# A depthwise convolution's partial sums for two of four channel tiles, added by accumulating transfers within SBUF in place of GpSimd additions

## The reference

```python
proj = h @ w_in
glu_in, qkv, gates = jnp.split(proj, [2 * CONV_WIDTH, 2 * CONV_WIDTH + 3 * ATT_WIDTH], axis=-1)
u_val, u_gate = jnp.split(glu_in, 2, axis=-1)
u = u_val * jax.nn.sigmoid(u_gate)
u = causal_depthwise_conv(u, conv_w, conv_b)      # 31 taps, 512 channels
u = jax.nn.silu(layernorm(u, conv_ln_g, conv_ln_b))
y_conv = u @ w_conv_out
...
o = stick_breaking_attention(qkv[:, :, 0], qkv[:, :, 1], qkv[:, :, 2])
...
merged = jax.nn.sigmoid(g_conv) * y_conv + jax.nn.sigmoid(g_att) * y_att
```

## Time and profile before

| | |
|---|---|
| time before, median of 3 runs | 1374.23 us (1372.99 to 1374.35) |
| profiled execution | 1373.22 us, span 1371.4 us |
| PE busy in the span | 1344.5 us (98%) |
| DVE busy | 986.8 us (72%) |
| ACT busy | 714.9 us (52%) |
| POOL busy | 180.9 us (13%), of it 105.7 us in the 60 sums |
| mean granted TensorE clock | 0.996 |

### The profile page before, as it was taken

The page is one execution under the profiler, slowest core; times in us unless marked ns, Lnnn a source line. Parts: engine busy times, 40 slices in busy tenths (PEclk is TensorE's granted clock), DMA queues, the critical chain, the costliest instruction groups (busy, mean ns, idle before and its releaser), DMA issues.

```text
span 1371.4 us, 19821 instructions
## 1 busy us (share of the span) xinstructions
PE 1344.5 (98%) x7788; PEld 1170.3 (85%) x7788; DVE 986.8 (72%) x1390; ACT 714.9 (52%) x1170; POOL 180.9 (13%) x167
## 2 busy tenths in 40 slices
PE   9999999999999999999999999999999999999997
PEld 7888888788769999998887778887778999998885
DVE  6799899678587878878326764677787788776322
ACT  4466886553475555573224543557465555564221
POOL 3388343200010000004000011121000000000000
PEclk9999999999999999999999999999999999999998
DMA  9422112455701332324532144543221323333221
GB/s 368 146 92 93 47 47 77 148 183 184 299 16 62 100 117 93 122 94 155 176 100 89 62 127 121 133 112 89 95 74 34 121 93 117 100 108 108 92 92 62
DMA packets 45310, 155.98 MB, mean 114 GB/s; under 512 B 6049, under 2 KB 6305, under 8 KB 45090
## 3 DMA queue, kind: packets, MB, share of 16 engines
q1 hardware_dynamic: 42882, 149.70, 32.9%
q0 software_dynamic: 2336, 5.01, 1.6%
HBM read 143.39 MB, written 2.10 MB: 106 GB/s over the span
## 4 chain that ended last, share of the span: by engine, by line
PE 88%; DVE 7%; ACT 3%; issue 1%; POOL 0%; DVEq 0%; ACTq 0%; POOLq 0%
PE ps L1741 27%; PE ps L1742 26%; PE ps L1743 26%; PE ps L1891 1%; DVE t_buf L1098 1%; PE ps L1829 1%; DVE w_lo L1064 1%; PE ps L2157 1%; PE ps L1783 1%; PE ps L1794 1%; PE ps L1795 1%; PE ps L1799 1%; DVE h_lo L1090 1%; ACT w_hi L578 1%; PE ps L2125 0%
## 5 line engine op out<-in xcount | busy, mean ns | idle before, releaser
L1741 PE MATMUL ps<-h_hi,w_hi 128*128 128x256 f32 (+1 forms) x1120 | 374.0, 334 | 3.0 <-ACT sq L806 1.1
L1743 PE MATMUL ps<-h_hi,w_lo 128*128 128x256 f32 (+1 forms) x1120 | 371.6, 332 | 0.0
L1742 PE MATMUL ps<-h_lo,w_hi 128*128 128x256 f32 (+1 forms) x1120 | 371.4, 332 | 0.0
L1064 DVE TENSOR_TENSOR w_lo<-raw,w_hi 128x1024 fp32r<-128x1024 f32 x141 | 183.7, 1306 | 115.6 <-ACT w_hi L578 114.4
L1741 PEld LDWEIGHTS ps<-h_hi,w_hi 128*128 128x128 f32 x1120 | 212.8, 190 | 27.1 <-issue 3.5
L1743 PEld LDWEIGHTS ps<-h_hi,w_lo 128*128 128x128 f32 x1120 | 212.8, 190 | 20.3
L1742 PEld LDWEIGHTS ps<-h_lo,w_hi 128*128 128x128 f32 x1120 | 212.9, 190 | 19.4 <-issue 0.5
L578 ACT ACTIVATE w_hi<-raw 128x1024 fp32r<-128x1024 f32 x141 | 148.1, 1055 | 147.1 <-PE ps L1743 74.0
L1054 DVE TENSOR_TENSOR w_lo<-quads,w_hi 128x1024 fp32r<-128x1024 f32 (+1 forms) x152 | 164.8, 1085 | 72.7 <-ACT w_hi L578 72.7
L578 ACT ACTIVATE w_hi<-quads 128x1024 fp32r<-128x1024 f32 (+1 forms) x152 | 144.3, 949 | 78.2 <-PE ps L1743 76.6
L1741 PE MATMUL ps<-act_hi,w_hi 128*128 128x512 f32 x352 | 137.0, 389 | 0.0
(11 more groups left out here) (316 smaller groups left out, 2262.3 us busy)
## 6 DMA issues: line engine op xcount, KB each, us to landing
quads<-in_ffn_in SPq DMA_DIRECT2D x76, 512.0 KB, 4.5
raw<-in_ffn_out SPq DMA_DIRECT2D x44, 512.0 KB, 3.7
raw<-in_ada SPq DMA_DIRECT2D x32, 512.0 KB, 4.2
raw<-in_qk SPq DMA_DIRECT2D x25, 512.0 KB, 3.7
ada<-in_ada SPq DMA_DIRECT2D x16, 512.0 KB, 7.6
raw<-in_gates SPq DMA_DIRECT2D x16, 512.0 KB, 3.7
raw<-in_v SPq DMA_DIRECT2D x12, 512.0 KB, 3.7
raw<-in_ffn_in SPq DMA_DIRECT2D x12, 512.0 KB, 3.9
```

Source lines behind the costliest of these rows:

```text
L1064: nc.vector.tensor_tensor(w_lo[SLOT[p]][:], raw[q % RAW][:], w_hi[SLOT[p]][:].bitcast(f32), ALU.subtract).then_inc(raw_used, 1)
L1741: nc.tensor.matmul(out, w[0], v[0], start=start, stop=False, **kw)
L1742: nc.tensor.matmul(out, w[0], v[1], start=False, stop=False, **kw)
L1743: return nc.tensor.matmul(out, w[1], v[0], start=False, stop=stop, **kw)
```

## The change

POOL no longer adds. For each of the 60 sums it issues a transfer from `tap_buf` to `conv`, both in SBUF, that adds what it brings to what stands there. The one counter `pool_tap` becomes two, `tap_sum[0]` for even n and `tap_sum[1]` for odd n, each raised by 16 when a transfer has landed; the same three waits (POOL's for the sum two places before, ACT's for the sum three places before, PE's for all sums) go to them. Order and number of the products, the three buffers and all other work stay.

```diff
-        mod_one, mod_ready, pool_tap = sem("mod_one"), sem("mod_ready"), sem("pool_tap")
+        mod_one, mod_ready = sem("mod_one"), sem("mod_ready")
+        tap_sum = [sem(f"tap_sum{i}") for i in range(2)]
...
             for n, (c, j) in enumerate(SUM_ORDER):
                 pool.wait_ge(tap_prod, n + 3)
                 if n >= 2:
-                    pool.wait_ge(pool_tap, n - 1)
-                nc.gpsimd.tensor_tensor(conv[:, c, :], conv[:, c, :], tap_buf[n % 3][:], ALU.add).then_inc(pool_tap, 1)
+                    pool.wait_ge(tap_sum[n % 2], 16 * (n // 2))
+                nc.gpsimd.dma_start(conv[:, c, :], tap_buf[n % 3][:], accum_op=ALU.add).then_inc(tap_sum[n % 2], 16)
...
                 for c, j in SUM_ORDER[tapped[0]:tapped[0] + n]:
                     if tapped[0] >= 3:
-                        act.wait_ge(pool_tap, tapped[0] - 2)
+                        act.wait_ge(tap_sum[(tapped[0] - 3) % 2], 16 * ((tapped[0] - 3) // 2 + 1))
...
                     pe.wait_ge(tap, len(TAP_ORDER))
-                    pe.wait_ge(pool_tap, len(SUM_ORDER))
+                    for i in range(2):
+                        pe.wait_ge(tap_sum[i], 16 * (len(SUM_ORDER) // 2))
```

## The result

The changed kernel takes 1404.37 us (median of 4 runs, 1398.62 to 1406.17) against 1373.64 us before (4 runs, 1372.99 to 1374.35): 2.2% slower, ratio 1.0216, 95% interval 1.0186 to 1.0247. The prediction was 1381.4 us, with a range from 1371.5 to 1399, so the result lies outside it. The sign was right and the size was not: the loss is 30.7 us where 7.2 were forecast.

What follows compares the result with a forecast made beforehand. PE was taken as the bound. -1.7 (wait for `qk_lo`) + 7.2 (late scores(1)) + 1.7 (clock) = +7.2 us on 1373.22 gave 1380.4; the runs' median, 1.0 higher, made it 1381.4, range 1371.5 to 1399.

Steps and rivals of the forecast that it cites:

- What bounds the kernel, and what can be gained: PE, busy 98% of the span, is the bound; only its 1.7 us wait for `qk_lo` can be gained.
- L: One link: time from an accumulating transfer's start of issue to the earliest issue of the next on the same tile.
- L alone, 3.9 us: Link of an undisturbed adding transfer, with 1.58 us of engine time charged for two passes: 3.9 us.
- L beside loads, 4.4 us: Link with two sums in flight and panels' loads holding 0.28 of the DMA engines: 4.4 us.
- a landing of 4.1 us: Sign in POOL's issue rows for `conv`: 4.1 us to land (L less 0.3) if the forecast is right.
- What L costs: In qk1 and v1, ACT falls behind; scores(1) begins at 83.8 + 14 L, 145.4 instead of 138.22: +7.2 us.
- The tail, hidden until L = 4.7: Last three sums on the odd tile end at 253.9, ahead of the mean at 254.81: no cost below L = 4.7.
- The clock, 1.7 us: Two new PE waits may cost one dip to half clock: between 0 and 3.4 us, 1.7 taken.
- hidden: Rival: L at most 4.0, adding costs no second engine pass, only DVE's relief is left: 1372.5 us, chance 0.36.
- The engines are the bound: Rival: DMA engines or POOL's issue bound, L 5.5 or more; at 5.6, 1401 us; chance 0.10.
- relief: DVE's taps, no longer slowed beside POOL's additions, end PE's wait for `qk_lo`: -1.7 us.
- the forecast's own formula: Start of scores(1) at 83.8 + 14 L us; each 0.1 us of L beyond 3.9 costs 1.4 us.

Runs made afterwards that it cites:

- experiment 3: Sums 33 to 53 by adding transfers, all others by GpSimd's additions as in the kernel before: 1371.87 us (11 runs), ratio 0.9987.
- experiment 2: The changed kernel with the panels from qk1 2 to gates 15 loaded in only 16 of 1024 columns: 1378.17 us in one run.
- experiment 8: The changed kernel with copies instead of additions and the loads from qk1 2 to gates 15 cut to 16 columns: 1373.83 us in one run.
- experiment 6: The changed kernel with 40 products of ones on PE right ahead of its wait for the last sums: 1403.0 us in one run.

## Why the prediction was right in sign and wrong in size

- **What bounds the kernel, and what can be gained:** right. PE's wait for `qk_lo` was the only gain, and it was half of what was forecast, 0.9 us for 1.7: DVE, freed of 2.3 us, next waits 1.3 us for ACT's `w_hi` (experiment 3).
- **L alone, 3.9 us:** right. It is 3.8 (experiment 2). The charge of 1.58 us of engine time for an adding transfer had the right size too: the page of the kernel before has, for the software queue,

```profile
q0 software_dynamic: 2336, 5.01, 1.6%
```

  so that in experiment 2 the 60 sums took 8.3% of 16 x 1376.3 us less 1.6% of 16 x 1371.4, which is 1477 us, or 1.54 us for each sum and engine, where 1.58 was forecast. A copy takes 0.69 (experiment 8, the same way, with a span of 1372.0 us). That the longer time is a second pass is not shown: the queue's bytes are the same for both, but an addition takes 144 packets, (10976 - 2336) / 60, and a copy 80, (7136 - 2336) / 60, so the smaller packets may be the reason as well. The 2.0 us plus bytes that the Trainium skill gives (DMA: Bandwidth & Descriptors, Anatomy of one DMA, SWDGE path), an estimate of 2.6 us here, lies between the landing of a copy (2.3 in experiment 8) and that of an addition (3.3 in experiment 2); the adding itself is not in it.
- **L beside loads, 4.4 us:** this is the step that failed. The trace has 5.0 over the first 11 links. 4.4 was the engine time that two sums need at a given share of loads, taken as the mean of L. That is only a floor for the rate; a transfer that meets a 512 KB load is late by itself (5.8 us to land from 91.55, with a load at 91.60, against 3.3 us in experiment 2), and the next sum of its tile cannot start meanwhile. Links of 3.8 to 7.0 us stand side by side. A mean share also takes the loads to be spread evenly, and they come in step with the sums. The sign that the prediction had named for being right, a landing of 4.1 us, is met by the page's median of 4.2: a median over all 60 hides the long ones, of up to 7.2 us.
- **What L costs:** the slope was right (14 links up to scores(1)). Between +7.2 and the 17.9 measured (19.4 less 1.5 of the start) 10.7 us were missed. Of these the first 11 links, at 4.97 for 4.4, are 6.3. The three behind the restart are 3.5: from the second sum of the pair (137.10 + 0.6) to product 32 at 154.41 they take 16.7 us, 5.6 each, where 13.2 were forecast. Some 0.9 are small steps between. The pair at the restart stands beside a load at 137.47; experiment 2 shows a long link at the same place with hardly any bytes of loads.
- **The tail, hidden until L = 4.7:** the limit was right, and L was over it: 263.06 + 0.6 to 283.5, three links of about 6.6 us. SP issues a load 0.4 to 0.5 us behind each of these three sums (264.04, 271.98 and 277.76), and in experiment 2, with few bytes of loads, the mean does not wait. 5.7 us for 0.
- **The clock, 1.7 us:** mis-sized: 4.5 behind scores(1) and 3.1 behind the mean, 7.6 in all. The second is shown to come from the wait (experiment 6), the first is read from the clock alone. The lower clock ahead of scores(1), 0.80 from 111 to 136 us, adds nothing to that: it lies inside the 17.9 us, and PE still had to wait at the end of them.
- **The rivals:** "hidden" fell. "The engines are the bound", with L = 5.6 and 1401 us, had the size, at a chance of 0.10, partly by luck: it had scores(1) at +24.0 us, where 17.9 were measured, and the tail and the clock too low, 2.7 and 1.7 for 5.7 and 7.6. But its reason, that loads and sums delay each other, is what the trace shows.

The mechanism was thus right, and the term that was mis-sized is L beside loads: 5.0 us over the first 11 links, 5.6 at the restart and 6.6 in the tail, for 4.4. Of the 30.3 us of the profile without the start's 1.5, 23.1 were missed: 10.7 up to scores(1), 5.7 in the tail, 5.9 of clock behind the two waits, and 0.8 of relief that did not come. By the forecast's own formula the mean of the 14 links, L = 5.1, gives 155.2 for scores(1), +17.0 us; with the tail's 5.7, the clock's 7.6 and the relief's 0.9 us it comes to +29.4.

## What to carry to other kernels

A chain of dependent transfers is priced by its slowest links beside the traffic that is really there, not by engine time at a mean share: here 3.8 us alone became 5.0, and the threshold lay between. Look also for what sets the traffic off: here the loads came in step with the sums. Before work is moved from an engine to transfers, ask how often the next step needs it: with a burst each 12.6 us the transfers were free and gave 0.13%, while the first 33, most of them with a burst each 5.4 us, cost some 23 us or 1.7%. And where a new wait lies in front of PE, add what the clock takes behind it: 3.1 and 4.5 us here behind waits of 5.7 and 6.7 us.

## What the runs showed of the hardware

- An adding transfer of 128 x 2 KB within SBUF kept each of the 16 engines busy for 1.54 us, a copy of the same bytes for 0.69 (both worked out from the queue's share), and POOL's issue of it took 0.85 us instead of 0.54.
- Issued 0.05 us ahead of a 512 KB load, such an adding transfer took 5.8 us to land; with few bytes of loads beside them 3.3 us was the median.
- A PE wait of 5.7 us ahead of the mean was followed by half clock for most of the next 6 us, one of 2.5 us by a shorter dip, and with PE kept busy instead the clock did not fall (6.70, 5.37 and 3.60 us for the same eight products).
